# Seven block products for the first two up blocks of every chunk, with token quadrants carried by squares on ACT

## What is computed

```python
def sqrelu_mlp(h, w_up, w_down):          # w_up 2048 x 8192, w_down 8192 x 2048
    u = jax.nn.relu(h @ w_up)
    return (u * u) @ w_down

for layer in range(DEPTH):                # DEPTH = 2
    h = rmsnorm(x, norm_mix_w[layer])
    x = x + mixer(h)                      # retention + RG-LRU, or attention
    h = rmsnorm(x, norm_mlp_w[layer])
    x = x + sqrelu_mlp(h, w_up, w_down)
return rmsnorm(x, final_norm_w)
```

## Time and profile before

| | us |
|---|---|
| median of 3 runs (lowest, highest) | 1993.55 (1993.31, 1994.81) |
| the profiled execution | 1995.09 |
| its span, first to last instruction | 1993.3 |
| PE busy | 1984.1 |
| DVE busy | 1581.1 |
| ACT busy | 1066.0 |
| granted clock of TensorE | 0.999 |
| HBM read | 379.34 MB, 191 GB/s |

### The profile page before, as it was taken

How to read it: one execution, slowest core, us unless ns; L and a number is a source line. 1 busy time by engine, 2 the same in 40 slices (tenths; PEclk the granted TensorE clock), 3 DMA queues, 4 the chain that set the end, 5 groups by cost and what they waited for, 6 DMA issues and landing times.

```text
span 1993.3 us, 25055 instructions
## 1 busy us (share of the span) xinstructions
PE 1984.1 (100%) x9089; PEld 1638.8 (82%) x9089; DVE 1581.1 (79%) x2190; ACT 1066.0 (53%) x1402; POOL 45.1 (2%) x55
## 2 busy tenths in 40 slices
PE   9999999999999999999999999999999999999998
PEld 7888888888888888888888878888888888888887
DVE  6777678989769868976889887989858876985875
ACT  6665665555445545544545566555445544544554
POOL 1110110000000000000000000000000000000000
PEclk9999999999999999999999999999999999999999
DMA  8556545655665475556655545564575555466563
GB/s 306 177 182 205 181 165 203 202 172 192 217 199 170 168 249 182 184 206 190 211 190 186 174 154 165 182 197 152 197 247 191 188 206 189 148 218 226 187 205 112
DMA packets 191758, 382.50 MB, mean 192 GB/s; under 512 B 6328, under 2 KB 7616, under 8 KB 191552
## 3 DMA queue, kind: packets, MB, share of 16 engines
q1 hardware_dynamic: 190288, 377.51, 56.5%
q0 software_dynamic: 1216, 3.88, 0.6%
q10 hardware_dynamic: 176, 0.07, 0.0%
HBM read 379.34 MB, written 2.10 MB: 191 GB/s over the span
## 4 chain that ended last, share of the span: by engine, by line
PE 98%; DVE 1%; issue 0%; ACT 0%; DMA 0%; ACTq 0%
PE acc L1399 26%; PE acc L1400 26%; PE acc L1401 26%; PE bank L1399 3%; PE bank L1400 3%; PE bank L1401 3%; PE acc L1426 1%; PE acc L1425 1%; PE acc L1427 1%; DVE area L1219 1%; PE bank L1427 1%; PE bank L1425 1%; PE bank L1426 1%; PE bank L1515 0%; PE bank L1592 0%; PE bank L1616 0%
## 5 line engine op out<-in xcount | busy, mean ns | idle before, releaser
L976 DVE TENSOR_TENSOR w_lo<-raw,w_hi 128x1024 fp32r<-128x1024 f32 x744 | 899.8, 1223 | 354.4 <-ACT w_hi L733 350.1
L733 ACT ACTIVATE w_hi<-raw 128x1024 fp32r<-128x1024 f32 x744 | 777.2, 1059 | 716.7 <-PE acc L1401 562.4
L1399 PE MATMUL acc<-w_hi,a_hi 128*128 128x512 f32 x1552 | 607.1, 391 | 0.0
L1401 PE MATMUL acc<-w_hi,a_lo 128*128 128x512 f32 x1552 | 604.1, 389 | 0.0
L1400 PE MATMUL acc<-w_lo,a_hi 128*128 128x512 f32 x1552 | 604.0, 389 | 0.0
L1399 PEld LDWEIGHTS acc<-w_hi,a_hi 128*128 128x128 f32 x1552 | 291.5, 188 | 61.2 <-issue 0.9
L1401 PEld LDWEIGHTS acc<-w_hi,a_lo 128*128 128x128 f32 x1552 | 291.4, 188 | 60.8
L1400 PEld LDWEIGHTS acc<-w_lo,a_hi 128*128 128x128 f32 x1552 | 291.4, 188 | 59.9
L1399 PE MATMUL acc<-w_hi,b_hi 128*128 128x512 f32 x784 | 305.7, 390 | 0.0
L1400 PE MATMUL acc<-w_lo,b_hi 128*128 128x512 f32 x784 | 305.3, 389 | 0.0
L1401 PE MATMUL acc<-w_hi,b_lo 128*128 128x512 f32 x784 | 305.0, 389 | 0.0
(11 more groups left out here) (240 smaller groups left out, 1296.8 us busy)
## 6 DMA issues: line engine op xcount, KB each, us to landing
raw<-in_mlp_w_up SPq DMA_DIRECT2D x128, 1024.0 KB, 5.4
raw<-in_mlp_w_down SPq DMA_DIRECT2D x128, 1024.0 KB, 5.1
raw<-in_hyb_w_in SPq DMA_DIRECT2D x44, 1024.0 KB, 5.3
raw<-in_attn_w_qkv SPq DMA_DIRECT2D x20, 1024.0 KB, 5.1
raw<-in_hyb_w_out SPq DMA_DIRECT2D x16, 1024.0 KB, 5.2
raw<-in_attn_w_out SPq DMA_DIRECT2D x16, 1024.0 KB, 5.1
raw<-in_hyb_w_in SPq DMA_DIRECT2D x5, 512.0 KB, 9.6
out_y<-x SPq DMA_DIRECT2D x4, 512.0 KB, 3.0
```

The source lines that it names most:

```text
L733: nc.scalar.activation(w_hi[:, ring(b, h)], raw[:, q, 2 * e:2 * e + 2, :], ACT.Copy).then_inc(hi_ready, 2 if what == ("R", HALVES - 1) else 1)
L976: nc.vector.tensor_tensor(w_lo[:, ring(b, h)], raw[:, q, 2 * e:2 * e + 2, :], w_hi[:, ring(b, h)].bitcast(F32), ALU.subtract).then_inc(lo_ ...
L1399: nc.tensor.matmul(a, xh, wh, start=first, stop=False, skip_group_check=joins)
L1401: ins = nc.tensor.matmul(a, xl, wh, start=False, stop=last, skip_group_check=joins)
```

## The change

The first two of the four up blocks of every chunk, in both MLPs and in all four chunks, now run as a pair too (`UP0`, `UP1`: eight pairs). Their first four k tiles are done by seven products from `a_hi`, `a_lo` and four sums of token tiles, `s_up`, that are made once per MLP (`add_up_tokens`) and copied again into `s_hi`, `s_lo` once a chunk (`up_tokens` on ACT, `up_tokens_rest` on DVE), since the down pairs use the same two tiles.

An up block's result has no `x` to be added to. Part results are copied to `part_l`, `part_r` in SBUF, and when a block of the pair is through, `sum_pair` on DVE adds the accumulator's two banks to them. `leave` on ACT waits for these sums (`pair_summed`) and reads the sums instead of PSUM.

For every up block, paired or not, the way to the turned tile is another: the squares now do the quadrants' move. ACT squares 16 pieces of 32 partitions x 256 columns from `stage` to `shifted`, each to another partition quadrant, at ticks 0, 1, 2 (4 + 6 + 6; two a tick at ticks 2 to 9 ahead of a down pair), and DVE turns `shifted` by 4 transposes of 128x256 instead of 16 of 32x256.

In an up pair the order of steps ends with the left block's L6, L7, then the empty step, then R4 to R7 of the right block: `leave` of the left block can run under the right block's last steps. The first MLP block is no longer woven with the second; L6 of the first pair of an MLP waits for the token tiles of the mixer's last block, which takes the spread ticks 6 to 9 and a tick more.

```diff
-BY_QUADRANT = {"up", "res"} | DIRECT
+BY_QUADRANT = {"res"} | DIRECT
+BY_VECTOR = BY_QUADRANT | {"up"}
+SQUARES_AT = {0: 4, 1: 6, 2: 6}
+SQUARES_PAIR = {2: 2, 3: 2, 4: 2, 5: 2, 6: 2, 7: 2, 8: 2, 9: 2}
...
+UP0 = {m + PERIOD * c for m in (MLP0, MLP1) for c in range(CHUNKS)}
+UP1 = {b + 1 for b in UP0}
+PAIRS0, PAIRS1 = UP0 | DOWN0, UP1 | DOWN1
+MIXED = [("P", 1), ("L", 2), ("P", 5), ("L", 3), ("P", 2), ("P", 6), ("P", 4), ("L", 4), ("P", 7),
+         ("L", 5), ("P", 3), ("R", 2), ("R", 3)]
+DOWN_STEPS = MIXED + [("R", 4), ("R", 5), ("R", 6), ("R", 7), (None, 0), ("L", 6), ("L", 7)]
+UP_STEPS = MIXED + [("L", 6), ("L", 7), (None, 0), ("R", 4), ("R", 5), ("R", 6), ("R", 7)]
...
@@ leave, on ACT
                 for tt in range(TT):
-                    src = acc[:, b % 2, tt, :]
+                    src = acc[:, ACC_OF[b], tt, :]
+                    if b in UP0 | UP1:
+                        act.wait_ge(pair_summed, slot.count(N_PAIR_SUMS, -1, tt + 1))
+                        src = (part_l if b in UP0 else part_r)[:, tt, :]
...
-                if kind == "up":
-                    for tt in range(TT):
-                        act.wait_ge(evac_act, slot.count(N_EVAC_ACT, -1, tt + 1))
-                        nc.scalar.activation(stage[:, tt, :], stage[:, tt, :], ACT.Square).then_inc(squared, 1)
+            def squares(slot, k):
...
+                if k == min(at):
+                    act.wait_ge(evac_act, slot.count(N_EVAC_ACT, 0))
...
+                for n in range(done, done + at[k]):
+                    a, f = divmod(n, QUADRANTS)
+                    ins = nc.scalar.activation(shifted[f * QUAD:(f + 1) * QUAD, a], src[a * QUAD:(a + 1) * QUAD, :, :, f, :],
+                                               ACT.Square)
+                if k == max(at):
+                    ins.then_inc(squared, 1)
...
@@ on DVE
+            def sum_pair(slot, b):
+                part = part_l if b in UP0 else part_r
+                dve.wait_ge(part_added, slot.pairs(4, 4, pair_of(b)[0]))
+                for tt in range(TT):
+                    nc.vector.tensor_tensor(part[:, tt, :], part[:, tt, :], accumulator(b, tt),
+                                            ALU.add).then_inc(pair_summed, 1)
...
+            def turn_shifted(slot, k):
+                if k != out_at("up", slot.b - 1) - 1:
+                    return
+                dve.wait_ge(turned_out, slot.count(N_TURNED, -1, INIT_HALVES))
+                dve.wait_ge(squared, slot.count(N_SQUARED, 0))
+                dst = turn.rearrange("p m (k t a c) -> p t (m k) a c", k=2, t=TT, a=QUADRANTS)
+                for a in range(QUADRANTS):
+                    ins = nc.vector.transpose(dst[:, :, :, a, :], shifted[:, a])
+                ins.then_inc(turned, 2)
...
@@ body, on PE
-                    if b in FIRST_PAIRS and k == LAST_TURNED_AT:
+                    if (b in FIRST_PAIRS and what == ("R", 6)) or (b in (MLP0, MLP1) and what == ("L", 6)):
                         pe.wait_ge(turned_out, slot.count(N_TURNED, 0, INIT_HALVES))
```

More of the change, by code:

```diff
@@ L125, with pair_of, unit_free, side_block @@
 SUM_COUNT = {5: 1, 7: 2, 6: 3, 4: 4}
-LAST_TURNED_AT = STEP_OF["R", 6]
+def pair_of(b):
+    first = b if b in PAIRS0 else b - 1
+    steps, units = (UP_STEPS, UP_UNITS) if first in UP0 else (DOWN_STEPS, DOWN_UNITS)
+    return first, steps, steps.index((None, 0)), units
+def unit_free(b, n):
+    _, steps, _, units = pair_of(b)
+    if n < 2:
+        return STEP_OF["P", 4 if n == 0 else 3] + 1
+    side, g = units[n]
+    return steps.index((side, 2 * g + 1)) + 1
+def side_block(b, side):
+    first = pair_of(b)[0]
+    return first + (side == ("R" if first in UP0 else "L"))
+LEFT = {side_block(b, "L"): (b in DOWN0 and b not in FIRST_PAIRS) for b in PAIRS0}
 WOVEN = ({MIX_OUT0, QKV0, ATT_OUT0}
          | {m + COLS * n for m in (MLP0, MLP1) for n in range(2 * CHUNKS)}) - PAIRS0
-NSTEP = [PAIR_SPLIT if b in PAIRS0 else len(PAIR_STEPS) - PAIR_SPLIT if b in PAIRS1 else HALVES
+NSTEP = [pair_of(b)[2] if b in PAIRS0 else len(pair_of(b)[1]) - pair_of(b)[2] if b in PAIRS1 else HALVES
          for b in range(NBLK)]
 STEP0 = [sum(NSTEP[:b]) for b in range(NBLK + 1)]
+def banks_of_blocks():
+    out, last = [], 1
+    for b in range(NBLK):
+        if b not in LEFT and not (b in DOWN0 and b not in FIRST_PAIRS):
+            last = 1 - last
+        out.append(last)
+    return out
+ACC_OF = banks_of_blocks()
 def ring(b, k):
@@ L148, in pair_step, with counts @@
 def pair_step(b, k):
[L150 to L154, removed]
+    if b not in PAIRS0 | PAIRS1:
+        return None
+    _, steps, split, _ = pair_of(b)
+    return steps[k + (split if b in PAIRS1 else 0)]
+def counts(b, k):
+    return 2 if b in PAIRS0 and k == NSTEP[b] - 1 else 1
 def weight_at(b, k):
@@ L240 @@
 SUMS_AT = {1: 0, 2: 1, 4: 2, 5: 3}
+N_PAIR_SUMS = [TT * sum(p < b for p in UP0 | UP1) for b in range(NBLK + 1)]
 N_EVAC_ACT = total(BY_ACT, TT)
@@ L398, in build @@
         place["at"] = 0
+        shifted = take(QUADRANTS, TT * NB // QUADRANTS).rearrange("p a (t k c) -> p a t k c", t=TT, k=COLS)
+        s_sum = take(4, 2, P)
+        s_up = take(4, 2, P)
+        part_l = take(TT, NB)
+        part_r = take(TT, NB)
+        place["at"] = 0
         kk_t = take(KV, SEQ)
@@ L848, in tokens, with up_tokens @@
                 nc.scalar.activation(s_hi[:, :, :, :], s_sum[:, :, :, :], ACT.Copy).then_inc(tokens_hi, 1)
+            def up_tokens(slot):
+                act.wait_ge(up_added, 1 if slot.b < MLP1 - 1 else 2)
+                if slot.b in DOWN0:
+                    act.wait_ge(half_used, slot.halves(STEP_OF["P", 3] + 1))
+                nc.scalar.activation(s_hi[:, :, :, :], s_up[:, :, :, :], ACT.Copy).then_inc(up_hi, 1)
             def post(slot, k):
```

142 lines of the change are left out of this document (94 added, 48 removed).

## The result

The changed kernel takes **2074.47 us** (median of 4 runs, 2073.05 to 2075.33) where the kernel before took 1993.59 beside it: a ratio of 1.0401, 95% interval 1.0388 to 1.0415. It is 4% slower, 81 us; 2038 had been forecast, with 2061 as upper end. Direction, mechanism and place were right, the size was not.

The account below looks back on a forecast made before the run. PE was taken to bound the kernel (busy 1984.1 of 1993.3 us), so late weights cost in full. 1995.1 - 8.2 + 36.4 + 16 = 2039.3, or a median of 2038 us, 2.2% slower; range 2014 to 2061.

Parts of the forecast that it names:

- PE's saving, -8.2: Eight up pairs lose 6 matmuls each; at 43.52 to 42.50 us a pair, 8.2 us less, all on the path.
- Durations: Instruction times on DVE and ACT: squares about 0.42 us, 128x256 transposes 0.44; busy ACT near 1275, DVE near 1540 us.
- some 50 us: How much lighter DVE as a whole was to get: 173 us less for transposes, 110 more for the pairs.
- The square from start to start, 0.323: A 32x256 square on ACT: nearest row's 0.418 us less 0.095 for overlap gives 0.323; bounds 0.26 to 0.40.
- my upper end of 0.40: Longest start-to-start time allowed for a square, in us; with it the chain came to +56 us instead of +36.4.
- The estimate with the 93 ns overlap: From the skill page's activation cost: a square takes 0.306 us start to start, stalls 4.4 instead of 4.9 us a chunk.
- 2.89: ACT's step behind a pair, six squares of 0.323 plus one w_hi cut of 0.95, in us, against 2.72 of PE.
- The chain, +36.4: Pair sums, leave and squares delay the weight cuts behind an up pair: 4.9 us in six chunks, 3.5 in two.
- The starts, +16: First up pair of each MLP, behind the mixer's last block: 8 us late each, +16 us; ends 11 to 18.
- At nothing: Terms priced at zero: copies instead of sums, leave from SBUF, the loads, and the other pairs' own steps.
- (A): Rival: the lead absorbs the added work, leaving only PE's saving, 1985.3 us; chance 9%.
- (D): Rival: PE's clock halves behind each 2.8 us pause for some 15 matmuls, 3 us more each, 2062 us; chance 5%.

Follow-up runs that it names:

- x5: Changed kernel with the squares behind each step's cut and those of the pair's second block spread over five steps, one step later: 2027.46 us.
- x7: Changed kernel with squares behind the cuts and each written to the partitions it reads, so output wrong: 2011.64 us.
- x3: Changed kernel with each square written to the partition quadrant it reads, same count, shapes and waits, output wrong: 2053.08 us.
- x14: Changed kernel with squares on the partitions they read plus ten idle matmuls in up 2's pause ahead of its fifth step, output wrong: 2048.91 us.
- x4: Changed kernel with 12 extra unused matmuls filling PE's long pause ahead of up 2's fifth step: 2073.42 us.
- x1: Changed kernel keeping the pairs but turning tiles as before, with two 128x512 squares on ACT and 16 transposes on DVE: 2086.32 us.

## Why the prediction was right and wrong

- **PE's saving, -8.2.** Right. In x5 and x7, where nothing is late in the pair, it runs in 42.49 to 42.51 us six times.
- **Durations.** The square was forecast at 0.42 and is 0.415; 128x256 transposes at 0.44 and are 0.41 (four in 1.42 us). Busy time came out at 1278 us against 1275 for ACT and 1515 against 1540 for DVE. The 1540, and the "some 50 us" by which DVE was to get lighter, don't follow from the prediction's own terms: 173 less and 110 more make 63, and 1518 us.
- **The square from start to start, 0.323: the step that failed.** I took the overlap of 0.095 from squares that follow each other in one quadrant for squares that each change it. That an instruction is a little longer than the distance to the next start, as the text ahead of the prediction has it for ACT and DVE, holds only there. The row that says otherwise stood beside it and was even used: three transposes, each to another quadrant than the one before, take 1.32 us at 0.436 each, that is 3 x 0.44 and no overlap. I booked 0.45 for them without asking why it wasn't 0.34. A square priced like its nearest row in kind, that transpose, costs its full duration, above my upper end of 0.40. The estimate with the 93 ns overlap of the Trainium skill's page "ScalarE: Activation LUTs" (What ACT_TABLE_LOAD costs) fell with it: squares behind one of the same quadrant follow it (0.30 to 0.33 for 0.306), the others don't. The cut was priced too low in the same way: behind it a square of another quadrant starts 1.08 to 1.09 us later and not 0.95. Together ACT's step is 3.65 and not 2.89. x3 takes it to 3.16 and the time down by 21.4 of the 36.5 us that were missed.
- **The chain, +36.4.** Its working was right in kind: place (up 2), releaser (w_lo), late steps (0, 1, 3, 4, the longest at 4) and the pair sums as its head. Measured as in the table it is 2.5 + 6.1 + 54.2 = 62.8 us, and 41.4 - 3.4 + 6.1 = 44.1 in x3. What the 7.7 us between 36.4 and 44.1 are isn't settled. The sum had no term for the clock (3 to 4 us by x14) nor for the restarts of 0.11 (29 waits for w_lo in x3, 3.2 us). But x3's step of 3.16 is also still 0.27 above the 2.89 of the sum, since quadrants change there too, between some squares and around most cuts; at the rate of x3 (18.6 us for 0.48 us a step) an estimate for that is 10 us.
- **The starts, +16.** 9.2 + 12.1, with the 1.0 of saving that each should have had and the 1.5 ahead of MLP 1, are 24.8: 8.8 more than forecast and above the end of 18. The waits stand where they were named (L6 1.6 us in MLP 0 and 3.2 in MLP 1, R2 1.9), but I had left out s_lo's wait at P5 and the first w_lo, and took the token sums ahead of MLP 1 to be hidden.
- **At nothing:** copies, loads and the other pairs: right, up 3 and the down pairs differ by 0.3 us in sum. `leave` from SBUF is a little slower: the first square follows 1.37 us behind its start where the timetable has 1.27, 0.1 us in each chain.
- **Rivals.** The lead didn't absorb it (A). The clock did fall (D), behind seven of the eight long pauses, with 5 to 12 matmuls at the lower level where 15 had been reckoned with, and was worth nothing measurable here: what I priced at 3 us a pause stands under ACT's own lateness (x4). That x1 lost more than the whole change shows that moving the turn to ACT was no mistake in itself; putting it ahead of the cuts was.

No version that was run beats the kernel before. The best whole one, x5, is 1.7% slower: in its chunks up 2 and the down pair lose more than the 1.02 us that a pair saves, and each start loses 8 to 9. Pairs only in the chunks behind the first, with squares that keep to a quadrant, would be some 4 us ahead by x7's blocks; that is an estimate, and no correct program of that form was tried.

## What to carry to other kernels

Ask for every run of short instructions whether each works in the same partition quadrant as the one before, and price it by a row that does likewise: the duration was nearly the same here, but the start-to-start distance was 0.427 against 0.31 us. An engine at 60% can still be what ends every wait, if its bursts stand ahead of what the bottleneck needs next; putting the urgent instruction first, and spreading the rest, gave 47 of 81 us back at no work saved. And price a pause by what the engine would have waited for anyway: a halved clock behind it cost nothing measurable here, and 3 to 4 us in x3, where the other engine was faster.

## What the runs showed of the hardware

- ACT overlaps an instruction with the next by some 0.09 us if both start in the same partition quadrant, and not at all if the next one reads or writes another. A 32x256 square from SBUF to SBUF is followed 0.30 to 0.33 us later within a quadrant (334 pairs in x3) and 0.41 later across (52 pairs). In the changed kernel, where each square writes another quadrant than the one before, it is 0.41 to 0.43 (386 pairs). A 128x1024 cut, which starts in quadrant 0, is followed 0.97 us later by a square that reads and writes quadrant 0 (6 in the changed kernel), 1.09 by one that reads quadrant 1 and writes 0 (32) and 1.09 by one that reads 0 and writes 2 (6): a change on either side is enough.
- VectorE's transposes are in line with that, though no run takes it apart for them: 0.44 apart when each goes to another quadrant, and four of 128x256, which all start in quadrant 0, in 1.42 us, so 0.34 apart.
- After a stall of PE the second matmul starts 0.31 to 0.34 us behind the first instead of 0.23, whatever the stall's length (0.34 at 0.63 us in the changed kernel and at 2.53 in x3), as long as the clock stays up.
- The changed kernel has 13 pauses of PE over 1.5 us in the MLPs. Behind nine of them (1.86 us the shortest) 5 to 12 matmuls ran at the lower level, 0.43 us apart; behind four, one of 3.0 us among them, none did, nor behind any of the short ones of 0.5 to 0.8 us. What tells them apart stays open. The drop needn't come at once: behind a pause of 1.86 us at the start of MLP 0 it is the fourth matmul that slows down.

```profile
411.02 0.49 PE L1551 MATMUL acc<-w_hi,a_hi 128*128 128x512 f32 x1 [1.86 <-DVE area L1102]
411.36 0.39 PE L1552 MATMUL acc<-w_lo,a_hi 128*128 128x512 f32 x1
411.59 0.44 PE L1553 MATMUL acc<-w_hi,a_lo 128*128 128x512 f32 x1
411.83 0.63 PE L1551 MATMUL acc<-w_hi,a_hi 128*128 128x512 f32 x1
412.25 0.63 PE L1552 MATMUL acc<-w_lo,a_hi 128*128 128x512 f32 x1
```
